# Third third of a ConvFFN down-projection: four of eight tiles by seven block products, the norm's first sums moved behind them

## The reference

```python
def layer_tail(x, mix, ffn_prev, p, ln_mg, ln_mb, ln_fg, ln_fb, w_up, conv_w, conv_b, w_down, w_proj, w_gate):
    h = layer_norm(ALPHA * x + mix, ln_mg, ln_mb)
    f, ffn_state = conv_ffn(h, ffn_prev, w_up, conv_w, conv_b, w_down)
    h = layer_norm(ALPHA * h + f, ln_fg, ln_fb)
    return h + jax.nn.sigmoid(h @ w_gate) * (p @ w_proj), ffn_state
```

## Time and profile before

| | us |
|---|---|
| median of 3 runs | 1587.85 |
| the three runs | 1585.98, 1587.87, 1587.85 |
| the profiled execution | 1586.58 |
| its span, first to last instruction | 1585.0 |
| TensorE busy in the span | 1547.0 |
| VectorE busy | 1108.6 |
| ScalarE busy | 755.7 |
| GpSimd busy | 341.7 |

### The profile page before, as it was taken

The page is one execution under the profiler, slowest core; times in us unless marked ns, Lnnn a source line. Parts: engine busy times, 40 slices in busy tenths (PEclk is TensorE's granted clock), DMA queues, the critical chain, the costliest instruction groups (busy, mean ns, idle before and its releaser), DMA issues.

```text
span 1585.0 us, 30823 instructions
## 1 busy us (share of the span) xinstructions
PE 1547.0 (98%) x12362; PEld 1510.5 (95%) x12362; DVE 1108.6 (70%) x1846; ACT 755.7 (48%) x1363; POOL 341.7 (22%) x670
## 2 busy tenths in 40 slices
PE   8999899998999999999999999999999999999999
PEld 8999787878999999999999999999999999999999
DVE  3336788874899756874567787868887568655684
ACT  4445677763455534433334536744553344334352
POOL 4702344420046013302110000001450222112000
PEclk9999999998999999999999999999999999999999
DMA  7636000052234134242232222232341343322312
GB/s 267 153 100 232 1 1 1 8 184 91 67 98 140 44 107 134 80 135 81 84 104 91 81 81 80 85 117 67 107 142 46 100 140 100 102 81 93 105 68 97
DMA packets 49934, 154.32 MB, mean 97 GB/s; under 512 B 6816, under 2 KB 15280, under 8 KB 49472
## 3 DMA queue, kind: packets, MB, share of 16 engines
q1 hardware_dynamic: 36864, 125.58, 24.3%
q0 software_dynamic: 12928, 26.77, 6.1%
HBM read 146.86 MB, written 9.10 MB: 98 GB/s over the span
## 4 chain that ended last, share of the span: by engine, by line
PE 87%; DVE 7%; ACT 3%; issue 2%; DMA 0%; POOL 0%; ACTq 0%; DVEq 0%
PE PS L2431 69%; PE PS L2797 3%; PE PS L2798 2%; PE PS L2799 2%; PE PS L2595 2%; PE PS L2557 1%; PE PS L2482 1%; PE PS L2483 1%; ACT ARENA L1042 1%; DVE SMALL L1605 1%; PE PS L2730 1%; PE PS L2548 1%; DVE LO L643 1%; DVE PTSL L1445 1%; DVE X L1911 1%
## 5 line engine op out<-in xcount | busy, mean ns | idle before, releaser
L2431 PE MATMUL PS<-XH,HI 128*128 128x272 f32 (+1 forms) x1744 | 367.0, 291 | 9.0 <-DVE XL L1445 8.3
L2431 PE MATMUL PS<-XH,LO 128*128 128x272 f32 (+1 forms) x1744 | 363.7, 289 | 0.0
L2431 PE MATMUL PS<-XL,HI 128*128 128x272 f32 (+1 forms) x1744 | 363.0, 289 | 0.0
L643 DVE TENSOR_TENSOR LO<-RAW,HI 128x1024 fp32r<-128x1024 f32 x217 | 266.0, 1227 | 109.6 <-ACT HI L638 107.5
L638 ACT ACTIVATE HI<-RAW 128x1024 fp32r<-128x1024 f32 x217 | 228.9, 1056 | 206.3 <-PE PS L2431 109.1
L2431 PEld LDWEIGHTS PS<-XH,HI 128*128 128x128 f32 x1744 | 277.0, 189 | 10.4 <-DVE LO L643 8.2
L2431 PEld LDWEIGHTS PS<-XL,HI 128*128 128x128 f32 x1744 | 276.1, 189 | 0.1
L2431 PEld LDWEIGHTS PS<-XH,LO 128*128 128x128 f32 x1744 | 275.0, 189 | 0.0
L2431 PE MATMUL PS<-GH,HI 128*128 128x272 f32 (+1 forms) x1312 | 273.8, 290 | 0.7 <-DVE LO L643 0.5
L2431 PE MATMUL PS<-GH,LO 128*128 128x272 f32 (+1 forms) x1312 | 271.3, 288 | 0.0
L2431 PE MATMUL PS<-GL,HI 128*128 128x272 f32 (+1 forms) x1312 | 270.9, 288 | 0.0
(11 more groups left out here) (426 smaller groups left out, 2530.4 us busy)
## 6 DMA issues: line engine op xcount, KB each, us to landing
RAW<-in_w_stream SPq DMA_DIRECT2D x211, 512.0 KB, 3.3
ARENA<-in_w_stream POOLq DMA_DIRECT2D x24, 256.0 KB, 4.5
ARENA<-in_w_stream SPq DMA_DIRECT2D x12, 512.0 KB, 4.5
ARENA<-in_cache_cmp POOLq DMA_DIRECT2D x32, 128.0 KB, 3.1
out_win_old<-in_win_copy POOLq DMA_DIRECT2D x1, 4064.0 KB, 18.0
X<-in_x SPq DMA_DIRECT2D x4, 544.0 KB, 6.8
X<-in_x POOLq DMA_DIRECT2D x1, 2176.0 KB, 8.5
ARENA<-in_cache_sel POOLq DMA_DIRECT2D x16, 128.0 KB, 3.0
```

What stands on the lines that cost most here:

```text
L643: nc.vector.tensor_tensor(LO[:, s * CH:(s + 1) * CH], split_source(c), HI[:, s * CH:(s + 1) * CH].bitcast(F32), ALU.subtract).then_inc(lo_ ...
L2431: ins = mm(PS[0:rows, b + h, 0:width], w[:, 0:rows], cols(part, h), start=first and len(parts) == 2 and n == 0, stop=last and len(parts) == 1)
```

## The change

`CROSSED` gets third 2 with the double 0: down tiles 0 to 3 of the third third are made by the fourteen products, tiles 4 to 7 stay plain under the name `rest`. `STEPS[(0,)]` is the part of `BOTH` with d = 0. Its banks are chosen anew in `SUM_BANKS`.

The plain tiles need B12 again where T1 stood. ScalarE therefore keeps B12 in SPARE (four copies in the up stage), writes its upper part into the operand behind `p3, 0`, and VectorE writes the lower parts, two behind `p3, 1` and two behind `p7, 1`. TensorE's rest tile 0 waits for them (`b12_lo`).

The norm's XS2 is made behind the last crossed product, its matmuls stand in rest tile 0 ahead of k = 4, and the centring, sums and pairs of all eight tiles are spread over the intervals of the last four. The load of PRAW, which GpSimd issued after the split of the second third's last `p4, 0` piece, is issued after that of the third third's. In both layers the work of block sums moves into the up stage of the third third too.

```diff
@@ -53,16 +53,16 @@
 
-CROSSED = {0: (1,), 1: (0, 1)}
+CROSSED = {0: (1,), 1: (0, 1), 2: (0,)}
 BOTH = ((0, "p1", 0), (0, "p1", 1), (0, "p5", 0), (0, "p5", 1), (0, "p2", 0), (0, "p2", 1), (0, "p6", 0), (0, "p3", 0),
...
         (1, "p7", 1), (1, "p3", 1), (1, "p4", 0), (1, "p4", 1))
-STEPS = {(0, 1): BOTH, (1,): ((1, "p1", 0), (1, "p1", 1)) + BOTH[-12:]}
+STEPS = {(0, 1): BOTH, (0,): tuple(x for x in BOTH if x[0] == 0), (1,): ((1, "p1", 0), (1, "p1", 1)) + BOTH[-12:]}
 DOUBLES = [(layer, t, d) for layer in (0, 1) for t in CROSSED for d in CROSSED[t]]
...
 OPENS = ("p1", "p2", "p5")
-SUM_BANKS = (((2, 3), (0, 1), (4, 5)), ((6, 7), (0, 1), (2, 3)))
+SUM_BANKS = (((2, 3), (0, 1), (4, 5)), ((6, 7), (0, 1), (2, 3)), ((0, 1), (2, 3), (4, 5)))
 INTO = {"p1": (0, 0), "p2": (0, 0), "p5": (1, 1), "p6": (0, 1), "p3": (0, 1), "p7": (1, 1), "p4": (1, 0)}
@@ -140,7 +140,7 @@
             piece_at[name, d, step, q] = x
-            where[name, d, step, q] = item("dve", None, (SUM_BANKS[d][SUM_OF[step]][q],), [x])
+            where[name, d, step, q] = item("dve", None, (SUM_BANKS[2 if ds == (0,) else d][SUM_OF[step]][q],), [x])
 
@@ -161,6 +161,8 @@
                 crossed(f"down{layer}{t}", ds)
+            if ds == (0,):
+                plain(f"rest{layer}{t}", 4, lambda n: "dve", one, lambda n: (n + 1) % 2)
         plain(f"proj{layer}", 8, lambda n: "act", lambda n: [n // 4], lambda n: (n + 1) % 2)
@@ -865,7 +868,7 @@
                     if t == max(CROSSED):
-                        pool.wait_ge(lo_ready, product_piece(layer, t, 1, "p4", 0) + 1)
+                        pool.wait_ge(lo_ready, product_piece(layer, t, CROSSED[t][-1], "p4", 0) + 1)
                         pool.dma_start(PRAW[:, :], a["p"][layer]).then_inc(p_landed, 16)
@@ -1142,15 +1145,21 @@
 
-                for k in range(KT):
+                def shift():
+                    act.wait_ge(shift_done, idx + 1)
+                    s.activation(halves(MP), PS[:, 4:6, 0:HALF], ACT.Copy, scale=4.0).then_inc(shift_took, 1)
+
+                parts = {4: (0, 1), 5: (2, 3, 4), 6: (5, 6)} if first else {2: (0, 1), 3: (2, 3), 4: (4,), 5: (5,), 6: (6,)}
+                for k in range(first, KT):
+                    if first and k == first:
+                        shift()
                     if k == 7:
...
                     if k == 2:
-                        act.wait_ge(shift_done, idx + 1)
-                        s.activation(halves(MP), PS[:, 4:6, 0:HALF], ACT.Copy, scale=4.0).then_inc(shift_took, 1)
-                    for m in {2: (0, 1), 3: (2, 3), 4: (4,), 5: (5,), 6: (6,)}.get(k, ()):
+                        shift()
+                    for m in parts.get(k, ()):
                         part(m)
@@ -1206,6 +1215,8 @@
                         s.activation(bh3[:, p % 8, :], PR_EVEN[:, 0:TOK], ACT.Copy).then_inc(mid_hi, 1)
+                        if CROSSED[p // 8] == (0,):
+                            s.activation(SPARE[p % 8 // 2], PR_EVEN[:, 2 * HALF:3 * HALF], ACT.Copy).then_inc(b12_kept, 1)
                     else:
@@ -1280,6 +1291,10 @@
                             splits.upto(IN_A_ROW[product_item(layer, t, d, step, q)] + SLOTS)
+                            if CROSSED[t] == (0,) and (step, q) == ("p3", 0):
+                                act.wait_ge(tile_done, product_item(layer, t, 0, "p5", 1) + 1)
+                                for j in range(4):
+                                    s.activation(bh3[:, 2 * j, HALF:TOK], SPARE[j], ACT.Copy).then_inc(b12_hi, 1)
                     elif t < 2:
@@ -1822,7 +1837,7 @@
                     dve.wait_ge(xs_ready, XS_PER_LN * idx + 1)
-                    dve.wait_ge(dve_took, taken(o0 + k)[1])
+                    dve.wait_ge(dve_took, taken(last if k < first else o0 + k)[1])
                     v.tensor_tensor(X3[:, k, :], X3[:, k, :], MP, ALU.subtract).then_inc(d_ready, 1)
@@ -1862,8 +1877,17 @@
                           6: ((ahead, 7), (total, 6), (lo, 5), (pair, 2), (lo, 6))}
-                for k in range(KT):
-                    if k < FUSED:
+                if first:
+                    beside = {4: ((centre, 2), (centre, 3), (ahead, 5), (total, 1), (total, 2)),
+                              5: ((ahead, 6), (total, 3), (total, 4), (pair, 0), (pair, 1)),
+                              6: ((ahead, 7), (total, 5), (total, 6), (pair, 2))}
+                    dve.wait_ge(dve_took, taken(last)[1])
+                    residual_sum(1)
+                    ahead(4)
+                    centre(0)
+                    centre(1)
+                for k in range(first, KT):
+                    if k < FUSED[idx]:
                         residual(o0 + k, k, scale)
@@ -2177,6 +2203,11 @@
                                 operand_lo(t, 3)
+                            elif CROSSED[t] == (0,):
+                                if (step, q) in (("p3", 1), ("p7", 1)):
+                                    for j in (0, 1) if step == "p3" else (2, 3):
+                                        dve.wait_ge(b12_hi, 4 * layer + j + 1)
+                                        sub_lo(bl3[:, 2 * j, HALF:TOK], SPARE[j], bh3[:, 2 * j, HALF:TOK], b12_lo)
                             elif (d, step, q) == (0, "p3", 1):
@@ -2196,7 +2227,7 @@
                 idx = 2 * layer + 1
-                centred(idx, down_item(layer, 2, 0), 1.0)
+                centred(idx, down_item(layer, 2, 0), 1.0, first=4, last=product_item(layer, 2, 0, "p4", 1))
                 for k in range(2):
@@ -2824,8 +2855,19 @@
                             one_product(t, 0, "p2", q, range(3, 4))
-                        for step in BOTH[6:]:
+                        for step in STEPS[CROSSED[t]][6:]:
                             one_product(t, *step)
+                        if CROSSED[t] == (0, 1):
+                            continue
+                        o0, c0 = O0[f"rest{layer}{t}"], C0[f"rest{layer}{t}"]
+                        for n in range(4):
+                            ready(o0 + n, c0 + n)
+                            for k in range(KT):
+                                if n == 0 and k % 2 == 0:
+                                    pe.wait_ge(b12_lo, 4 * layer + k // 2 + 1)
+                                if n == 0 and k == 4:
+                                    beside(2 * layer + 1, 2)
+                                products(o0 + n, c0 + n, k, bh3, bl3, k, k == 0, k == 7)
                         continue
@@ -2836,8 +2878,6 @@
                         tile(o0 + n, c0 + n, range(KT), bh3, bl3, 0)
-                        if t == 2:
-                            beside(2 * layer + 1, n)
                     if is_half(t):
...
                             one_product(t, *step)

```

More of the change, by code:

```diff
@@ L350, in build @@
         s2_summed, s3_summed, s4_summed = sem("s2_summed"), sem("s3_summed"), sem("s4_summed")
+        b12_kept, b12_hi, b12_lo = sem("b12_kept"), sem("b12_hi"), sem("b12_lo")
         t1_sum, t1_hi, t1_lo = sem("t1_sum"), sem("t1_hi"), sem("t1_lo")
@@ L403, in build @@
         MID_COUNT = {"ffn0": 1, "ln2_0": 25, "rec": 33, "gated": 41, "ffn1": 49, "ln2_1": 73}
-        XS_PER_LN, FUSED = 8, 3
+        XS_PER_LN, FUSED = 8, (3, 4, 3, 4)
         PROD0 = (2, 2 + 24 + 8 + 2)
@@ L559, in down_item @@
         def down_item(layer, t, n):
-            return O0[f"down{layer}{t}"] + n
+            return O0[f"rest{layer}{t}"] + n - 4 if CROSSED.get(t) == (0,) else O0[f"down{layer}{t}"] + n
         def product_item(layer, t, d, step, q):
@@ L1131, in _, with centred @@
             s.activation(SMALL[:, 509:510], SMALL[:, 1:2], ACT.Copy).then_inc(phase_end, 1)
-            def centred(idx, o0, layer=None):
+            def centred(idx, o0, layer=None, first=0):
                 def part(k):
-                    if k < FUSED:
-                        act.wait_ge(d_ready, FUSED * idx + k + 1)
+                    if k < FUSED[idx]:
+                        act.wait_ge(d_ready, sum(FUSED[:idx]) + k + 1)
                     else:
@@ L1291, in tail @@
                 idx = 2 * layer + 1
-                centred(idx, down_item(layer, 2, 0))
+                centred(idx, down_item(layer, 2, 0), first=4)
                 def proj(k):
@@ L1815, in param_columns, with centred @@
                     v.tensor_tensor(col(bl), src, col(bh).bitcast(F32), ALU.subtract).then_inc(gb_ready, 1)
-            def centred(idx, o0, scale, layer=None):
+            def centred(idx, o0, scale, layer=None, first=0, last=None):
                 def residual_sum(_):
@@ L1833, in total @@
                 def total(k):
-                    if k < FUSED:
-                        dve.wait_ge(d_ready, FUSED * idx + k + 1)
+                    if k < FUSED[idx]:
+                        dve.wait_ge(d_ready, sum(FUSED[:idx]) + k + 1)
                     else:
@@ L2042, in product @@
                     out = product_halves(p)
+                    if CROSSED.get(p // 8) == (0,) and p % 8 in (2, 4, 6):
+                        dve.wait_ge(b12_kept, 4 * layer + p % 8 // 2)
```

## The result

The change makes the kernel slower: median 1597.71 us (4 runs, 1596.7 to 1598.5) against 1586.91 before on the same chip (4 runs), ratio 1.007 with a 95% interval from 1.0057 to 1.0082. The profiled execution took 1596.7 us. The forecast was 1592.0, from 1586.5 to 1595: the sign was right, the loss over twice as large as forecast.

What follows compares the result with a forecast made beforehand. The prediction took TensorE, 98% busy, to bound the kernel. Terms of +2.37 us per layer, +4.7 in all, gave 1591.3 from the profiled 1586.58; set between two bases, the forecast was 1592.0, range 1586.5 to 1595.0.

Steps and rivals of the forecast that it cites:

- second new wait: Third third, at p4, 1: TensorE waits because VectorE's split of rest tile 1 waits for its load; +1.45 us per layer.
- What goes: Third third's down-projection: 168 matmuls replace 192 on TensorE, taking 3.01 us per layer off the path.
- the start of the products: Short waits before the twelfth product, copied from the second third, +0.79 us per layer; work moved into the up stage free.
- First new wait: Third third, at p7, 1: TensorE waits because VectorE's split of rest tile 0 waits for its load; +1.30 us per layer.
- Third new wait: At the norm's shift in rest tile 0: TensorE waits for the sum behind VectorE's splits and takings; +1.84 us per layer.
- The norm beside four tiles: VectorE's norm work squeezed beside four tiles instead of six: last add on time, charged 0, with no slack.
- The sum: All terms per layer added: -3.01 + 0.79 + 1.30 + 1.45 + 1.84 = +2.37 us; two layers +4.7 us.
- The rule on transfers: Rest tile 1's load sharing engines with PRAW's would land about 1.0 us later, adding some 2 for two layers; not used.
- (a): Rival: TensorE's saved work comes off one for one, -4.5 us, about 1582 to 1583; chance 0.12.
- (b): Rival: the waits in the third third are there but smaller, 0 to +3 us, 1587 to 1590.5; chance 0.28.
- (c): Rival: the norm spills, last add 0.9 us late; with a later load +3.5 per layer, 1594 to 1595; chance 0.10.

Runs made afterwards that it cites:

- the run with the sum first: The change with VectorE's sum for the norm's shift directly behind the last taking, rest 0's split after some takings, rest 1 to 3's after the sum; 1581.42 us.
- the run with only the sum moved: The change with p loaded earlier and the shift's sum put ahead of the splits of rest 2, 3 and p's lower part; 1585.61 us.
- the run with the early load of p: The change with p loaded earlier, into EXT, and the store of the conv rows moving with it; 1590.22 us.

## Why the prediction was wrong, by its own steps

The step that failed is one term of the second new wait, the length of the load of rest tile 1; a second term, the clock, was missing.

- **What goes, and the start of the products:** right. -3.01 + 0.79 is the stage of the run with the sum first, to 0.02 us. The work moved into the up stage costs nothing: from the last add of layer 0 to that of layer 1 the change takes 670.26 us against 664.95, 5.31 more, and the third third of layer 1 alone accounts for 5.32.
- **First new wait:** right in place and cause; 0.96 and 1.13 against 1.30. Its load took 3.2 and 3.3 where 3.5 was taken.
- **Second new wait:** right in place and cause, wrong in size, and this is the step that failed. "So I take 4.3: landed 19.64, VectorE's split starts at 20.74." It took 7.2, the split started at u = 23.63 and p4, 1 at 26.01 instead of 23.12: 2.9 us later, exactly the 2.9 by which the load was late. In layer 1 it took 6.3, and p4, 1 came 2.0 later. The row behind the 4.3 has one transfer beside the load; here there were GpSimd's two, and 2.6 us behind it SyncE's load of rest 2. That last one alone does not make the load late: in the run with only the sum moved it went out 2.5 us behind in both layers, and the load took 4.3 and 3.2. The store stood in the prediction's own sentence and got no price. With the store out of the way layer 1 took 4.1, and its stage came to 50.96 where the sum says 51.0.
- **The clock:** a term that was missing. The longer idle time let the granted clock fall. p4, 1 at half rate is 12 matmuls x about 0.11 us longer, its operand places come free later, ScalarE's upper part of rest 3 and with it the sum are later. The forecast had the load of rest 3 decide there. The shift is at u = 33.41 where 29.48 was forecast: 2.9 from the load and 1.0 from this. In layer 1 it is 2.0 + 0.9. The gap at the shift is shorter for it, which is why of the 2.2 us at the lower level only 1.1 are left in the stage.
- **Third new wait:** as a gap smaller (0.54 and 1.12 against 1.84), since the second had already held TensorE. Where the second wait was of the forecast size it is 1.84, and with nothing of GpSimd's queue beside the loads 1.89 and 2.01.
- **The norm beside four tiles:** right. The second to last add is 0.5 late and the last on time in every version.
- **The sum:** forecast +2.37 per layer, measured +6.39 and +5.32. Load late by 2.9 and 2.0, and 1.1 and 1.0 behind that, is the whole difference. The two stages alone would take the profiled execution from 1586.58 to 1598.3; it took 1596.7, by the 1.6 us less ahead of them, which the change does not touch.
- **The rule on transfers** (the Trainium skill, DMA: Bandwidth & Descriptors, Bandwidth: 1 MB in 6.15 us) was put aside for the row. By it, with the store counted, 512 + 544 + 432 KB from 816.4 end about 9 us later, at 825; the load landed at 824.7. That they meet is no proof of the rule here: 1 MB in 6.15 us is about 170 GB/s, while the DMA engines moved 2.43 MB in the 8 us from 816 to 824, 304 GB/s, part of it the load of rest 2, which is not in this sum. What the runs show is the price of each neighbour: 4.1 with the load of p, 6.3 with the store as well (both layer 1).
- **Rivals.** (a), TensorE's work off one for one, was wrong for this order; the kernel with the sum first, 1581.4, comes out half a microsecond better than its 1582 to 1583. The prediction excluded it with "even with loads of no length VectorE's chain alone would bring the shift at about 25.7, 0.8 behind TensorE": true of this order, and no bound on what the step can give. (b) is nearest to the run with the early load of p, 1590.2. (c) is at work in none.

## What to carry to other kernels

On an engine that works in order, put first what the busiest engine needs next, and a split that waits for a load behind it: here one such reordering turned +11 us into -5 with the same transfers. When a wait hangs on a load, list every transfer issued within its time on all queues, stores too, and take a row with as many beside it. To move takings alone only moves the wait; count what stands behind each blocked instruction until nothing that TensorE needs is left.

## What was not expected of the hardware

The 512 KB load of rest tile 1 took 3.2 to 3.6 us with nothing from GpSimd's queue beside it (4.3 in layer 0 of two kernels), 4.1 and 5.8 beside one load of 544 KB, and 5.8 to 7.6 with a store of 432 KB as well. In layer 0 it was longer than in layer 1 in each of the seven kernels that cross the third third, by 0.3 to 1.8 us. An instruction packet lay beside it in layer 0 each time and in layer 1 never.

The packet shows more plainly beside loads that nothing else accompanies. In the ten traces 916 loads of 512 KB into RAW ran with no other transfer under way. The 609 without an instruction packet in their time took 3.1 to 3.6 us; of the 307 with one or two, 69 took longer, up to 5.2 us. One of these, from the kernel before (DMA view of 830 to 836 us):

```profile
q8 instruction: 1, 0.02, 2.1%
...
RAW<-in_w_stream SPq DMA_DIRECT2D x1, 512.0 KB, 5.1
```

So a lone load of over 3.6 us always had such a packet beside it, while most packets delayed nothing. That the packet is the cause is the reading that fits; no run moves it.

In these third thirds TensorE's gaps of 3.13, 3.56, 4.61, 6.13 and 7.92 us were each followed by some 5 us in which the granted clock was 0.50 to 0.69 on average, while behind the gaps of up to 2.0 us it was 1.00. After 3.56 us it was

```profile
1498.67:1503.20 4.53, 4.53 (x24) 4.53 (x25) 3.00 (x6) 1.56 (x2) 0.00 (x0) 0.62 0.62 203
```

that is 24 matmuls in the time of 36, some 1.5 us on top of the wait itself.
